# Compressed scores of an attention branch: keys held still on four column strips, scores turned back, and one low-weight subtraction moved behind two softmax steps

## The chip, the cores and the metric

The kernel runs on one core of one Trainium2 chip. TensorE multiplies matrices into PSUM, VectorE (DVE in the rows) and ScalarE (ACT) do elementwise work, GpSimd (POOL) some products, SyncE (SP) issues most transfers. The metric is the device time of one execution in microseconds. Before the change it is 2274.6 us, the median of three runs (2272.6 to 2280.66).

## The reference

Two transformer blocks over 256 tokens of width 1024. The first is a layer with three branches: a gated linear recurrence (A), a sparse attention (B), a gated linear attention (C). They are merged as

```
gates = sigmoid(merge_logit)                    # from h, one gate row per branch
merged = gates[0] * (y_a @ w_branch[0]) + gates[1] * (y_b @ w_branch[1]) + gates[2] * (y_c @ w_branch[2])
```

Branch B has 16 heads in 4 key groups, head width 64. For each head it sums three attentions: over the selected blocks, over the window, and over 15 compressed keys, which a small network makes from blocks of 32 tokens. The last one is what the change touches:

```
logit_c = einsum("bgrsd,bgcd->bgrsc", q, kc) + bias_c
p_c = softmax(where(valid_c, logit_c, NEG_INF)) * valid_c
o_cmp = einsum("bgrsc,bgcd->bgrsd", p_c, vc)
```

The second block (adaptive norms, two attention layers, gated feed-forward layers) is not touched.

## The kernel before

Each engine has one instruction stream, written out by hand, and the streams meet at semaphores. Weights are streamed into a ring in SBUF. A product of large weights is made in three passes of a one-pass type: ScalarE rounds a half chunk of 128x2048 weights to its high part (`w_hi`, L1656), VectorE subtracts to make the low part (`w_lo`, L2299), and TensorE multiplies high by high, high by low, low by high (`split_part`, L938 to L940). `rests_last` (L954, L955, L959) does the same 48 matmuls in another order: the 32 that need only the high weights come first, then a wait for the low weights, then the 16 with them.

Products in plain f32 (scores, turns, compressed network) leave two records each in the profile; a turn leaves one.

The stretch in question lies at 312 to 342 us. Branch C's last merge step, `mergeC3`, stands in the order after the start of branch B's attention (the postponed step): its half 0 is the gate logits (from h), its half 1 is y_c times w_branch. Around it:

- TensorE: small matmuls of the compressed network end (L1388 to L1410); `scores(0, 0)`, `scores(0, 1)` for unit 0 (L1281; a unit is a key group and a tile of 128 tokens); `compressed()` (L1423), 16 matmuls with the queries as the stationary 128x128 and only 14 or 30 key columns moving; `scores(1, 0)`, `scores(1, 1)`; `late_half(0, True)` by `split_part`; `late_half(1, False)` by `rests_last`; then the first turns and products of units 0 and 1 (L1326, L1352). `scores(1, 0)` may start when two of the four exponentials of unit 0 are through (`att_exp` at 2), `scores(1, 1)` at 4. The first product of L1352 waits until VectorE has emptied half 1 (`merged("C", 3)`).
- VectorE: `att_max(0)` (L2883, L2884), `w_lo` for half 0, `cmp_max(0)` and `cmp_max(1)` (L2914 to L2916: bias, maximum, subtraction), `att_max(1, (0,))` (L2877), `att_norm(0)` (L2936 to L2949), `w_lo` for half 1, `cmp_norm(0)` (L2923 to L2927), `att_max(1, (1,))`, `cmp_norm(1)`, `att_norm(1)`, `merged("C", 3)` (L2625, L2626), and then the next unit's `att_max`.
- ScalarE: exponentials of unit 0 (L2011), two `w_hi`, exponentials of the compressed scores (L2019), parts 0 and 1 of unit 1's exponentials, a table load and the sigmoid of the gate half (`late_gate`, L1853), a table load, parts 2 and 3 of unit 1's exponentials, which wait for `att_max(1, (1,))`.
- PSUM banks: raw scores of a unit 0 to 3, compressed scores 4, `late_half(0)` 5 and 6, `late_half(1)` 7 and 4.

Of the kernel before, what the change touches and what calls it, by code (L numbers as in the profile page):

```python
# [19 lines left out]
P = 128  # L20
D = 1024
KT = D // P
S = 256
# [10 lines left out]
CMP_N = S // 16 - 1  # L34
# [7 lines left out]
BANK = 512  # L42
# [275 lines left out]
def cmp_keys(t):  # L318

    return CMP_N if t else CMP_N // 2  # L320
# [17 lines left out]
def build(nc, d, out_x):  # L338
    f32 = mybir.dt.float32
    ACT = mybir.ActivationFunctionType  # L340
    ALU = mybir.AluOpType
    AX = mybir.AxisListType.X
    ctx = ExitStack()
    with ctx:
# [42 lines left out]
        def V(name, a=0, n=None):  # L387
            at, w = VOFF[name]
            return vec[:, at + a:at + (w if n is None else a + n)]
# [5 lines left out]
        def area(at, *shape):  # L395

            n = int(np.prod(shape))
            assert at + n <= ARENA, (at, shape)
            v = arena[:, at:at + n]
            if len(shape) == 2:  # L400
                return v.rearrange("p (a b) -> p a b", a=shape[0])
            if len(shape) == 3:
                return v.rearrange("p (a b c) -> p a b c", a=shape[0], b=shape[1])
            return v
# [8 lines left out]
        def cmp_scores(t):  # L413

            return psum[:, CMP_AT + cmp_col(t, 0):CMP_AT + cmp_col(t, 16)]

        def by_head(a):

            return a.rearrange("p (h c) -> p h c", h=16)
# [69 lines left out]
        def sig(name):  # L489
            if name not in sems:  # L490
                sems[name] = ctx.enter_context(nc.semaphore(name))
            return sems[name]
# [59 lines left out]
        B_pc = area(B_T_at + 4096, 16 * cmp_keys(0)), area(10916, 16 * cmp_keys(1))  # L552
        B_stat = [area(11156 + 16 * i, 16) for i in range(6)]
        B_hid = area(B_hid_at, 2, 2, 60)
        B_kd = V("wa2", 0, 8 * CMP_N).rearrange("p (g b c) -> p g b c", g=4, b=2)
        B_vc = area(10660, 4, HD)
        B_hT = rr[:, :].rearrange("p (i n) -> p i n", i=2)
        B_PT = area(16384, 3, BANK)
# [324 lines left out]
        def _(pe):  # L883
# [46 lines left out]
            def split_part(h, b, at, xh, xl, done, before=None, both=False, ks=None, between=None):  # L930

                wh, wl, nk = half_weights(h)
                ks = range(nk) if ks is None else ks
                for c, k in [(c, k) for k in ks for c in range(2)] if both else [(c, k) for c in range(2) for k in ks]:
                    if before is not None and c == 0:
                        before(k)
                    whc, wlc = wh[:, k, c * P:(c + 1) * P], wl[:, k, c * P:(c + 1) * P]
                    mm(b[c][:, at], whc, xh[:, k, at], start=(k == ks[0]), stop=False)  # L938
                    mm(b[c][:, at], whc, xl[:, k, at], start=False, stop=False)  # L939
                    last = mm(b[c][:, at], wlc, xh[:, k, at], start=False, stop=(k == ks[-1]))  # L940
                    if k == ks[-1] and done is not None:
                        last.then_inc(done, 1)
                    if k == ks[-1] and c == 0 and between is not None:
                        between()
# [320 lines left out]
            def scores(u, a):  # L1265
                kind, g, t = UNITS[u]

                def free(b):

                    if u > 0:  # L1270
                        pe.wait_ge(sig("att_exp"), 4 * (u - 1) + b + 1)

                if kind == "nsa":
                    nk = P * (t + 1)
                    free(1 + 2 * a)
                    for seg in range(2):
                        for r in (2 * a, 2 * a + 1):
                            half = slice(64 * (r % 2), 64 * (r % 2) + 64)
                            kk = (B_kk if g % 2 == r % 2 else B_ks)[half, 2 * seg + g // 2, 0:nk]
                            at = place(seg, r) * S  # L1280
                            last = mm(psum[:, at:at + nk], B_q[half, 2 * g + r // 2, t * P:(t + 1) * P], kk,  # L1281
                                      start=True, stop=True)
                else:
                    ev = kind == "ev"
                    k0 = S if t >= 2 else 0
                    for r in (2 * a, 2 * a + 1):
                        h = 4 * g + r
                        half = slice(64 * (r % 2), 64 * (r % 2) + 64)
                        free(r)
                        if ev:  # L1290
                            q = E_qk[half, h // 2, t * P:(t + 1) * P]
                            kk = (E_qk[half, 4, k0:TOK] if g == r % 2 else E_ks[half, k0:TOK])
                        else:
                            q = O_q[half, h // 2, t * P:(t + 1) * P]
                            kk = O_k[half, h // 2, 0:TOK]
                        last = mm(psum[:, r * BANK + k0:(r + 1) * BANK], q, kk, start=True, stop=True)  # L1296
                last.then_inc(sig("att_score"), 1)
# [117 lines left out]
                wait_evac(pe, TILE["cmp_kv"] + 1)  # L1415
                pe.wait_ge(sig("kswap_in"), 32)

            def compressed():
                for t in range(2):
                    sc = by_head(cmp_scores(t))  # L1420
                    for g in range(4):
                        for j in range(2):
                            last = mm(sc[:, 4 * g + j:4 * g + 4:2, :], B_q[:, 2 * g + j, t * P:(t + 1) * P],  # L1423
                                      B_kd[:, g, :, 0:cmp_keys(t)], start=True, stop=True)
                last.then_inc(sig("cmp_score"), 1)

            def late_half(half, both_parts):
                h = HALF_AT[f"mergeC3_{half}"]
                b = [late_tile(half, j) for j in range(2)]
                if both_parts:  # L1430
                    split_part(h, b, slice(0, S), h_hi, z_lo, filled)
                else:
                    pe.wait_ge(sig("cmp_exp"), 2)
                    rests_last(h, b, slice(0, S), C_yh, C_yl, filled)
# [1 line left out]
            nsa_ready()  # L1436
            scores(0, 0)
            scores(0, 1)
            compressed()
            scores(1, 0)  # L1440
            scores(1, 1)
            late_half(0, True)
            late_half(1, False)
# [831 lines left out]
        def _(dve):  # L2275
# [3 lines left out]
            def link(ins):  # L2279

                steps[0] += 1
                ins.then_inc(sig("dve_step"), 1)
                dve.wait_ge(sig("dve_step"), steps[0])
# [7 lines left out]
            def w_lo(h):  # L2291

                if h < lo_made[0] or h >= len(HALVES):
                    return
                assert h == lo_made[0]
                lo_made[0] += 1
                at = half_slot(h)
                dve.wait_ge(sig("w_hi"), h + 1)
                v.tensor_tensor(out=ring_r[:, at], in0=ring[:, at],  # L2299
                                in1=W_hi[h % NHI][:, 0:HALVES[h][2]].bitcast(f32), op=ALU.subtract)\  # L2300
                    .then_inc(sig("w_lo"), 1)
# [607 lines left out]
            def cmp_max(t):  # L2909
                n, nm = cmp_keys(t), B_stat[t]  # L2910
                sc = by_head(cmp_scores(t))
                bc = B_stage[:, :, 0:16 * (n - 1) + 1:16][:, :, ::-1]
                dve.wait_ge(sig("cmp_score"), 1)
                link(v.tensor_tensor(out=sc, in0=sc, in1=bc, op=ALU.add))  # L2914
                link(v.reduce_max(nm, sc, AX, negate=True))
                v.tensor_tensor(out=sc, in0=sc, in1=rep(nm, n), op=ALU.add).then_inc(sig("cmp_max"), 1)  # L2916

# [39 lines left out]
            def att_done(u, y):  # L2957
# [14 lines left out]

            link(v.memset(B_kd, 0.0))
            b = empty(TILE["cmp_kv"])
            v.tensor_copy(B_kd[0:64, :, 0, :], b[0:64, 0:60].rearrange("p (g c) -> p g c", g=4))
            v.tensor_copy(B_kd[64:128, :, 1, :], b[64:128, 0:60].rearrange("p (g c) -> p g c", g=4))\
                .then_inc(evac["V"], 1)
            b = empty(TILE["cmp_kv"] + 1)
            v.tensor_copy(B_vc[0:CMP_N, :, :], b[0:CMP_N, 0:256].rearrange("p (g d) -> p g d", g=4))\
                .then_inc(evac["V"], 1)  # L2980
            dve.wait_ge(sig("stage_in"), 16)
            att_max(0, (0, 1))
            w_lo(HALF_AT["mergeC3_0"])
            cmp_max(0)
            cmp_max(1)
            for u in range(0, NSA_U[1], 2):
                att_max(u + 1, (0,))
                att_norm(u, B_P, B_y)
                if u == 0:
                    w_lo(HALF_AT["mergeC3_1"])  # L2990
                    cmp_norm(0)
                att_max(u + 1, (1,))
                if u > 0:
                    att_done(u - 1, B_y)
                    if u + 2 < NSA_U[1]:
                        att_max(u + 2, (0,))
                    att_norm(u + 1, B_P, B_y)
                else:
                    cmp_norm(1)
                    att_norm(1, B_P, B_y)  # L3000
                    merged("C", 3, lambda j: late_tile(1, j))
                    att_max(2, (0,))
                    att_done(0, B_y)
                if u + 2 < NSA_U[1]:
                    att_max(u + 2, (1,))
                if u > 0:
                    att_done(u, B_y)
# [389 lines left out]
```

## Time and profile before

| | us |
|---|---|
| median of three runs | 2274.6 |
| the profiled execution | 2274.26 |
| its span, first to last instruction | 2272.5 |
| TensorE busy | 2240.5 (99%) |
| VectorE busy | 1456.9 (64%) |
| ScalarE busy | 929.2 (41%) |

The profile's busy time of TensorE runs to the modelled end of each matmul, so it says little on how full the array is; which engine sets the pace of a stretch is read from what each engine waits for there. The profile also lists the TensorE clock that was granted: 1.00 of full speed (2.4 GHz) in nearly the whole span, 0.50 (1.2 GHz) in one stretch, which is the one of this change.

### The profile page before, as it was taken

The numbers are of one execution on the slowest core, as the hardware profiler recorded it, in microseconds if no ns is written. First come the engines' busy times: TensorE is split into PE (matmuls) and PEld (weight loads), VectorE is DVE, ScalarE is ACT, GpSimd is POOL, SyncE is SP. The second block draws the span as 40 slices with busy tenths as digits, with TensorE's granted clock in tenths as the row PEclk, the third lists the DMA queues.
The fourth block names the chain that finished last, engine by engine and source line by source line (L and its number), as shares of the span: only waits on it lengthen the run. The fifth ranks groups of instructions, "written<-read, shape, count | busy, mean of one in ns | idle before, by whom it ended". The sixth has DMA issues, their size and how long they took to land.

```text
span 2272.5 us, 33457 instructions
## 1 busy us (share of the span) xinstructions
PE 2240.5 (99%) x14230; PEld 1958.4 (86%) x14230; DVE 1456.9 (64%) x1968; ACT 929.2 (41%) x1338; POOL 286.3 (13%) x254
## 2 busy tenths in 40 slices
PE   8999999999999999999999999999999999999999
PEld 8999986999998888888769888889888888978999
DVE  7674567788777767757858676326655332987554
ACT  7854447454552122234544212224322222556443
POOL 2020105121102010100110101000100101202111
PEclk9999999999999999999999999999999999999999
DMA  7553461756544545323213544223454321623553
GB/s 293 186 202 145 151 228 45 262 210 261 193 166 172 213 157 222 145 85 124 79 38 149 202 168 185 74 93 149 153 218 164 132 102 68 180 97 112 186 186 112
DMA packets 35728, 358.23 MB, mean 158 GB/s; under 512 B 4237, under 2 KB 6477, under 8 KB 9212
## 3 DMA queue, kind: packets, MB, share of 16 engines
q1 hardware_dynamic: 32124, 343.54, 40.3%
q0 software_dynamic: 3456, 12.56, 1.9%
q8 instruction: 112, 1.84, 0.3%
q14 instruction: 36, 0.29, 0.0%
HBM read 353.11 MB, written 1.13 MB: 156 GB/s over the span
## 4 chain that ended last, share of the span: by engine, by line
PE 91%; DVE 4%; ACT 3%; issue 1%; DMA 0%; POOLq 0%; ACTq 0%; DVEq 0%
PE psum L938 25%; PE psum L939 25%; PE psum L940 24%; PE psum L1031 2%; PE psum L1030 2%; PE psum L1029 2%; PE psum L959 1%; PE psum L954 1%; PE psum L955 1%; PE psum L1352 1%; PE psum L1326 1%; ACT arena_r L1656 1%; DVE ring_r L2299 1%; PE psum L1296 1%; PE psum L1281 1%
## 5 line engine op out<-in xcount | busy, mean ns | idle before, releaser
L938 PE MATMUL psum<-arena_r 128*128 128x256 f32 (+2 forms) x3032 | 1021.7, 337 | 4.5 <-DVE arena_r L2645 2.8
L940 PE MATMUL psum<-arena_r,ring_r 128*128 128x256 f32 (+2 forms) x3032 | 1015.5, 335 | 0.0
L1656 ACT ACTIVATE arena_r<-ring 128x2048 fp32r<-128x2048 f32 (+1 forms) x252 | 473.6, 1881 | 674.1 <-PE psum L940 619.9
L939 PE MATMUL psum<-zT_r,arena_r 128*128 128x256 f32 (+1 forms) x2240 | 741.3, 331 | 0.0
L2299 DVE TENSOR_TENSOR ring_r<-ring,arena_r 128x2048 fp32r<-128x2048 f32 (+1 forms) x251 | 569.0, 2269 | 187.7 <-ACT arena_r L1656 187.0
L938 PEld LDWEIGHTS psum<-arena_r 128*128 128x128 f32 x3032 | 570.6, 188 | 78.5 <-DVE ring_r L2299 4.1
L940 PEld LDWEIGHTS psum<-arena_r,ring_r 128*128 128x128 f32 x3032 | 573.0, 189 | 63.2
L939 PEld LDWEIGHTS psum<-zT_r,arena_r 128*128 128x128 f32 x2240 | 420.6, 188 | 41.8
L939 PE MATMUL psum<-arena_r 128*128 128x256 f32 (+2 forms) x1240 | 405.7, 327 | 0.0
L2455 DVE CUSTOM_DVE_ANT_0 psum<-arena,cb 128x1024 f32<-128x1024 f32 x256 | 315.7, 1293 | 0.0
L939 PEld LDWEIGHTS psum<-arena_r 128*128 128x128 f32 x1240 | 234.3, 189 | 22.2
L838 POOL TENSOR_TENSOR arena_r<-rt,arena_r 128x512 fp32r<-128x512 f32 (+1 forms) x55 | 81.7, 1486 | 990.6 <-ACT arena_r L1757 990.6
L2387 DVE SCALAR_TENSOR_TENSOR xT<-psum,gates_h,xT 128x256 f32<-128x256 f32 x168 | 75.4, 480 | 128.8 <-PE psum L940 128.0
L2521 DVE TENSOR_TENSOR rr<-psum,rr 128x512 f32<-128x512 f32 (+1 forms) x53 | 31.2, 590 | 175.4 <-PE psum L940 175.4
L2521 DVE TENSOR_TENSOR rt<-psum,rt 128x512 f32<-128x512 f32 (+1 forms) x53 | 31.3, 590 | 151.3 <-PE psum L940 149.5
L838 POOL TENSOR_TENSOR arena_r<-rr,arena_r 128x512 fp32r<-128x512 f32 (+1 forms) x55 | 78.7, 1432 | 343.6 <-ACT arena_r L1757 343.6
L938 PE MATMUL psum<-xT_r,arena_r 128*128 128x256 f32 x384 | 109.1, 284 | 0.7 <-DVE ring_r L2299 0.7
L940 PE MATMUL psum<-xT_r,ring_r 128*128 128x256 f32 x384 | 108.5, 283 | 0.0
L1031 PE MATMUL psum<-arena_r,zT_r 128*128 128x256 f32 x336 | 94.4, 281 | 0.0
L1029 PE MATMUL psum<-arena_r 128*128 128x256 f32 x308 | 87.8, 285 | 0.0
L1030 PE MATMUL psum<-ring_r,arena_r 128*128 128x256 f32 x308 | 86.3, 280 | 0.0
L1778 ACT ACTIVATE rt<-psum 128x512 f32<-128x512 f32 (+1 forms) x53 | 27.5, 519 | 139.0 <-PE psum L940 116.1
(386 smaller groups left out, 2470.7 us busy)
## 6 DMA issues: line engine op xcount, KB each, us to landing
ring<-in_wf SPq DMA_DIRECT2D x75, 2048.0 KB, 7.7
ring<-in_w SPq DMA_DIRECT2D x40, 2048.0 KB, 7.7
arena<-in_w SPq DMA_DIRECT2D x73, 1024.0 KB, 9.6
ring<-in_wf SPq DMA_DIRECT2D x10, 1536.0 KB, 6.4
ring<-in_w SPq DMA_DIRECT2D x6, 1024.0 KB, 8.7
arena<-strip_scratch POOLq DMA_DIRECT2D x1, 2048.0 KB, 10.4
arena<-rpb_scratch POOLq DMA_DIRECT2D x16, 128.0 KB, 10.7
xT<-in_x SPq DMA_DIRECT2D x1, 1024.0 KB, 7.1
```

The costliest lines, as they stand in the source:

```text
L838: pool.tensor_tensor(out=lo[:, i, :], in0=a, in1=hi[:, i, :].bitcast(f32), op=ALU.subtract)\
L938: mm(b[c][:, at], whc, xh[:, k, at], start=(k == ks[0]), stop=False)
L939: mm(b[c][:, at], whc, xl[:, k, at], start=False, stop=False)
L940: last = mm(b[c][:, at], wlc, xh[:, k, at], start=False, stop=(k == ks[-1]))
L1029: mm(b, xh[:, k, at], wh[:, k, :], start=(k == 0), stop=False)
L1030: mm(b, xh[:, k, at], wl[:, k, :], start=False, stop=False)
L1031: last = mm(b, xl[:, k, at], wh[:, k, :], start=False, stop=(k == nk - 1))
L1656: A(W_hi[h % NHI][:, 0:n], ring[:, half_slot(h)], ACT.Identity).then_inc(sig("w_hi"), 1)
L2299: v.tensor_tensor(out=ring_r[:, at], in0=ring[:, at], in1=W_hi[h % NHI][:, 0:HALVES[h][2]].bitcast(f32), op=ALU.subtract)\
L2387: return v.scalar_tensor_tensor(out=xT[:, k, at], in0=b[:, at], scalar=gate(k, s), in1=xT[:, k, at], op0=ALU.mult, op1=ALU.add)
L2455: v.tensor_tensor_reduce(out=psum[:, at:at + D], in0=src[:, b * D:(b + 1) * D], in1=cb[:, s * D:(s + 1) * D], scale=1.0, scalar=0.0, op0=A ...
L2521: v.tensor_tensor(out=a, in0=b[:, 0:nt], in1=a, op=ALU.mult).then_inc(evac["V"], 1)
```

## The change

Compressed scores. Instead of queries stationary and 14 or 30 key columns moving, each group's compressed keys become a stationary operand of 32 columns (two head parities by 16, the 16th key column zero), placed on column strip 32g of the array, and 256 tokens of queries move: 8 matmuls, into bank 7. The scores then lie keys by tokens. VectorE copies the bank to SBUF (`B_sc`, 128x512), TensorE turns it back in four 128x128 transposes into bank 7, and the addition of the bias reads from there, in two instructions for each token tile instead of one, and writes where the scores were before. In TensorE's order the turns come between `scores(1, 0)` and `scores(1, 1)`.

The postponed step. Half 0 uses `rests_last` instead of `split_part`, and VectorE makes its low weights after `cmp_max(0)`, `cmp_max(1)` and `att_max(1, (0,))` instead of before them.

```diff
-        B_kd = V("wa2", 0, 8 * CMP_N).rearrange("p (g b c) -> p g b c", g=4, b=2)
+        B_kd = V("wa2", 0, 8 * 16).rearrange("p (g b c) -> p g b c", g=4, b=2)
+        B_sc = area(24064, BANK)
+        cmp_flat = psum[:, 7 * BANK:8 * BANK]
...
-            def compressed():
+            def compressed_by_key():
+                for j in range(2):
+                    for g in range(4):
+                        last = mm(cmp_flat[32 * g:32 * g + 32, j * S:(j + 1) * S],
+                                  B_kd[:, g, :, :].rearrange("p b c -> p (b c)"), B_q[:, 2 * g + j, :],
+                                  start=True, stop=True, tile_position=(0, 32 * g))
+                last.then_inc(sig("cmp_by_key"), 1)
+
+            def compressed_turned():
+                pe.wait_ge(sig("cmp_copied"), 1)
                 for t in range(2):
-                    sc = by_head(cmp_scores(t))
-                    for g in range(4):
-                        for j in range(2):
-                            last = mm(sc[:, 4 * g + j:4 * g + 4:2, :], B_q[:, 2 * g + j, t * P:(t + 1) * P],
-                                      B_kd[:, g, :, 0:cmp_keys(t)], start=True, stop=True)
+                    for j in range(2):
+                        at = t * S + j * P
+                        last = nc.tensor.transpose(cmp_flat[:, at:at + P], B_sc[:, j * S + t * P:j * S + (t + 1) * P],
+                                                   C("ident"))
                 last.then_inc(sig("cmp_score"), 1)
...
-                    split_part(h, b, slice(0, S), h_hi, z_lo, filled)
+                    rests_last(h, b, slice(0, S), h_hi, z_lo, filled)
...
-            compressed()
+            compressed_by_key()
             scores(1, 0)
+            compressed_turned()
             scores(1, 1)
...
-                link(v.tensor_tensor(out=sc, in0=sc, in1=bc, op=ALU.add))
+                for j in range(2):
+                    at = t * S + j * P
+                    turned = cmp_flat[:, at:at + P].rearrange("p (h c) -> p h c", h=8)
+                    link(v.tensor_tensor(out=sc[:, j::2, :], in0=turned[:, :, 0:n], in1=bc[:, j::2, :], op=ALU.add))
...
             att_max(0, (0, 1))
-            w_lo(HALF_AT["mergeC3_0"])
+            dve.wait_ge(sig("cmp_by_key"), 1)
+            v.tensor_copy(B_sc, cmp_flat).then_inc(sig("cmp_copied"), 1)
             cmp_max(0)
             cmp_max(1)
             for u in range(0, NSA_U[1], 2):
                 att_max(u + 1, (0,))
+                if u == 0:
+                    w_lo(HALF_AT["mergeC3_0"])
                 att_norm(u, B_P, B_y)
```

## Rows read from the trace of the kernel before

**Rows 1.** The page, part 4: shares of the chain that ended last, by engine.
```profile
PE 91%; DVE 4%; ACT 3%; issue 1%; DMA 0%; POOLq 0%; ACTq 0%; DVEq 0%
```

**Rows 2.** Stretches: length; busy us of PE, PEld, DVE, ACT, POOL; granted clock; DMA.
```profile
312.60:316.30 3.70, 2.33 (x24) 1.82 (x24) 0.85 (x3) 2.19 (x5) 0.00 (x0) 1.00 0.96 319
...
317.40:320.00 2.60, 2.60 (x22) 2.59 (x20) 2.53 (x5) 2.59 (x9) 0.00 (x0) 0.83 1.00 429
320.00:322.85 2.85, 2.85 (x14) 2.80 (x14) 2.11 (x1) 2.85 (x11) 0.00 (x0) 0.50 1.00 425
...
326.28:328.00 1.72, 1.72 (x16) 1.72 (x15) 1.65 (x9) 1.11 (x5) 0.66 (x1) 1.00 0.02 5
```

**Rows 3.** Order of time, TensorE: start, us, line, operands, records, idle time before.
```profile
205.59 1.92 PE L1211 MATMUL psum<-arena 128*32 128x256 f32 x16
...
221.41 1.91 PE L1211 MATMUL psum<-arena 128*32 128x256 f32 x8
...
317.41 5.52 PE L1423 MATMUL psum<-vec,arena 128*128 128x14 f32 x32
322.86 3.49 PE L1281 MATMUL psum<-arena 64*128 64x256 f32 x16
...
326.29 0.39 PE L938 MATMUL psum<-xT_r,arena_r 128*128 128x256 f32 x1
...
337.73 0.60 PE L1326 MATMUL psum<-cst,arena 128*128 128x128 f32 x4
...
340.56 0.65 PE L1352 MATMUL psum<-arena 128*64 128x256 f32 x4 [0.57 <-DVE zT L2626]
...
343.54 1.14 PE L1281 MATMUL psum<-arena 64*128 64x256 f32 x8
344.61 0.66 PE L1326 MATMUL psum<-cst,arena 128*128 128x128 f32 x4
```

**Rows 4.** Order of time, VectorE, 319.8 to 340.1 us.
```profile
319.83 2.28 DVE L2299 TENSOR_TENSOR ring_r<-ring,arena_r 128x2048 fp32r<-128x2048 f32 x1
322.97 0.35 DVE L2914 TENSOR_TENSOR psum<-psum,arena 128x112 f32<-128x112 f32 x1 [0.86 <-PE psum L1423]
...
325.23 0.42 DVE L2877 CUSTOM_DVE_ANT_0 psum<-psum,arena 128x256 f32<-128x256 f32 x1
...
326.72 0.20 DVE L2936 RECIPROCAL small<-small 128x8 f32<-128x8 f32 x1
...
327.83 3.13 DVE L2299 TENSOR_TENSOR ring_r<-ring,arena_r 128x2048 fp32r<-128x2048 f32 x1
330.89 0.26 DVE L2923 TENSOR_REDUCE arena<-arena 128x16 f32<-128x112 f32 x1
...
333.66 0.14 DVE L2877 DVE_READ_ACCUMULATOR2_ANT small<- 128x1 f32 x1
333.66 0.40 DVE L2923 TENSOR_REDUCE arena<-arena 128x16 f32<-128x240 f32 x1
...
335.94 0.20 DVE L2936 RECIPROCAL small<-small 128x8 f32<-128x8 f32 x1 [0.50 <-ACT arena L2011]
...
340.09 0.42 DVE L2626 TENSOR_TENSOR zT<-zT,rt 128x256 f32<-128x256 f32 x1
```

**Rows 5.** Order of time, ScalarE: exponentials of units 0 and 1, a table load.
```profile
319.93 0.22 ACT L2011 ACTIVATION_READ_ACCUMULATOR arena<-psum,small 128x1 f32 x1
...
332.68 1.28 ACT L2011 ACT_TABLE_LOAD   x1
333.98 0.47 ACT L2011 ACTIVATE arena<-psum,small 128x256 f32<-128x256 f32 x1
```

**Rows 6.** Line 2914 alone: its two instructions, shortest, median, longest in ns.
```profile
L2914 DVE TENSOR_TENSOR psum<-psum,arena x2: 355/462/570, 323.0 to 323.9; 128x112 f32<-128x112 f32 x1, 128x240 f32<-128x240 f32 x1
```

**Rows 7.** Groups at 305 to 352 us: busy us, mean ns, idle before.
```profile
L2883 DVE TENSOR_TENSOR psum<-psum,arena 128x512 f32<-128x512 f32 x4 | 2.8, 693 | 0.9 <-PE psum L1281 0.9
L2967 DVE COPY arena<-psum 128x256 f32<-128x256 f32 x2 | 0.8, 425 | 2.4 <-PE psum L1352 2.4
```

More of the change, by code:

```diff
@@ L2974, in _ @@
             b = empty(TILE["cmp_kv"])
-            v.tensor_copy(B_kd[0:64, :, 0, :], b[0:64, 0:60].rearrange("p (g c) -> p g c", g=4))
-            v.tensor_copy(B_kd[64:128, :, 1, :], b[64:128, 0:60].rearrange("p (g c) -> p g c", g=4))\
+            v.tensor_copy(B_kd[0:64, :, 0, 0:CMP_N], b[0:64, 0:60].rearrange("p (g c) -> p g c", g=4))
+            v.tensor_copy(B_kd[64:128, :, 1, 0:CMP_N], b[64:128, 0:60].rearrange("p (g c) -> p g c", g=4))\
                 .then_inc(evac["V"], 1)
```

## The prediction

> **What bounds the kernel now.** First the page's chain: 91% of it is TensorE [rows 1], so over the span a microsecond off TensorE's path is a microsecond off the end. But the change lies in 20 us where the engines hand work to each other, so the stretch has to be read by itself. The table of stretches shows the granted clock there: at 312.6 to 316.3 us TensorE does little, at full clock; in the stretch from 317.4 the mean is 0.83, and from 320.0 on it is 0.50, the lower level of 1.2 GHz; at 326.28 it is 1.00 again [rows 2]. Before it fell the engine had stood nearly idle, then done unit 0's scores and half of the narrow matmuls of L1423.
>
> TensorE in order of time: L1423 from 317.41 to 322.86, 5.45 us; `scores(1, ...)` 3.4 us to 326.29, mostly at the lower clock; then 96 matmuls of the postponed step to 337.73, 0.119 us each; turns and scores; and at 340.56 the first product, for which TensorE waited on VectorE's L2626 [rows 3]. That wait ends the stretch: everything behind it on TensorE (`scores(2, 1)`), VectorE (`att_max(2)`) and ScalarE follows from it. So the question is what moves 340.51, the end of L2626 [rows 4].
>
> Back from there. L2626 ends 4.57 us after `att_norm(1)` begins at 335.94, and that began when ScalarE's exponentials of unit 1, begun at 333.98, were through: VectorE was idle 0.50 us before it [rows 4, 5]. Those exponentials wait for two things: the table load at 332.68, which ends at 333.96, and `att_max(1, (1,))`, which VectorE ended at 333.66 + 0.14 = 333.80 [rows 4, 5]. The first hangs on TensorE (the sigmoid needs the gate half, which ended near 332.0), and VectorE's line stood only 0.18 us behind it. Taking time from TensorE alone can gain next to nothing here; what adds over 0.18 us to VectorE's line is late at the end.
>
> **The change part by part.** (1) The compressed matmuls. 5.45 us of L1423 go. In their place are 8 f32 matmuls, 16 records, of 32 stationary columns and 256 moving. The nearest row is L1211, the same shape: 8 records on one strip take 1.91 us, 16 records on two strips 1.92 [rows 3], so two strips run beside each other. Bounds for 16 records over four strips: 3.8 us if all go in single file, 1.0 us if four go abreast; I take 1.0 to 1.9, so the end is at 318.4 to 319.3. Either way it is hidden, since `scores(1, 0)` cannot start until two exponentials of unit 0 are through, at 319.93 + 0.22 = 320.15 [rows 5], about 320.3 on TensorE. L1423 had covered that wait; now it lies open, and 5.45 us removed bring `scores(1, 0)` forward by 322.86 - 320.3 = 2.6 us.
>
> (2) The copy. VectorE is through with `att_max(0)` at 319.83, when its first subtraction began before [rows 4]. The copy of 128x512 out of PSUM has no row; a copy half as wide takes 0.43 us, an addition of the same width 0.69 [rows 7]. I take 0.69, as time follows width: done at 320.5. It could cost 0.43 at best. Queued behind it is `cmp_max`, which waits for the turns.
>
> (3) The turns. `scores(1, 0)` at full clock takes 344.61 - 343.54 = 1.07 us, four turns 0.66 [rows 3]: 320.3 + 1.07 + 0.66 = 322.0. VectorE begins `cmp_max` at 322.05 and not 322.97. It has stood idle for 1.5 us, where the subtraction of 2.28 us stood before.
>
> (4) `cmp_max` took 325.23 - 322.97 = 2.26 us [rows 4]. Each of its additions is now two. From 355 ns for 112 elements and 570 for 240 [rows 6] a line gives 1.68 ns an element and 167 ns fixed; one more fixed part and hand-over each time is 0.2 us, twice: 2.66 us, to 324.7. The bound below is nothing, if the fixed parts overlap.
>
> (5) `att_max(1, (0,))`, 326.72 - 325.23 = 1.49 us: to 326.2. Now the moved subtraction, 2.28 us as before, since no GpSimd work is beside it: to 328.5. (Beside GpSimd the other one takes 3.13 [rows 4], which is its bound above.) `att_norm(0)`, 1.11 us: 329.6. The second subtraction with GpSimd beside it, 3.06: 332.65. `cmp_norm(0)` and `att_max(1, (1,))`, 2.77 + 0.14: 335.55. So the exponentials begin at 335.6 and not 333.98, `att_norm(1)` at 335.6 + 1.96 = 337.6 and not 335.94, and L2626 ends at 342.1 and not 340.51: **+1.6 us**.
>
> The same in one line: copy 0.69, idle 1.53, second additions 0.4, less the idle 0.86 that is gone, less the slack 0.18, is +1.6.
>
> (6) TensorE meanwhile. The postponed step starts at about 323.1 and not 326.29, 3.2 us sooner. Its 32 high matmuls end at 323.1 + 3.8 = 326.9; then it waits until 328.5 for the low weights; the 16 last end at 330.4; half 1 (low weights there at 332.65) ends at 336.1, 1.6 us sooner than 337.73. `rests_last` delays the first of the gate's two tiles, but both sigmoids and the table load behind them still end near 332.6, ahead of 335.6. Then turns and scores until the third turn, which needs ScalarE's first copy, behind the exponentials, at 338.2; TensorE is out of work at 338.8 and stands until 342.1, 3.3 us against 0.57 before [rows 3]. All that TensorE saves is given back in this wait.
>
> (7) For nothing: B_kd's wider memset, the changed views of its copies, and the load that SyncE issues when half 1 ends, which comes sooner; no engine waits for these here.
>
> **The sum.** The profiled execution took 2274.26 us (span 2272.5), 0.3 below the median of 2274.6. With +1.6 it is 2275.9, on the median 2276.2. About 0.5%, 11 us, is what a measurement of this kernel can tell from no change: its three runs lie 8 us apart.
>
> **The rivals.** (A) The lower clock again falls on this stretch. For it: it did, and the idle time before 316.3 is untouched. Against: the narrow matmuls are gone. `scores(1, 0)` and the turns would take up to twice 1.73 us, so `cmp_max` begins 1.2 to 1.7 later: +2.8 to +3.3, 2277.7.
>
> (B) A second low stretch, slower. TensorE's new idle time of 3.3 us before 342.1 is nearly as long as that of 312.6 to 316.3, after which the clock fell. It decides if the clock falls before the dense work of unit 2. Price by the one such stretch: 16 records of scores took 3.4 us there against 2.1, so 1.3 us, and up to 3.4 if it lasts as long as before and all is TensorE's. On top of 1.6: 2277.5 to 2279.6. The Trainium skill, TensorE: Matmul & The Clock Gate, section "Why this matters for your kernels", warns that an idle gap between bursts of matmuls returns the clock to its lower level. By that rule (B), or (A), is what happens; the one fall in this trace agrees with it, since it follows the idle stretch, and the 0.57 us wait at 340.56 was followed by none.
>
> (C) The strips do not run beside each other, because four write one bank. Then 3.8 us, or about 5.9 if the clock falls midway: `cmp_max` begins 0.9 to 4.7 later than in (3), +2.5 to +6.3: up to 2280.9. Against: the two strips of L1211.
>
> (D) Faster: TensorE's line sets the end and not VectorE's. For it: the table load that bound ScalarE hung on TensorE, and a copy of 0.43, an addition split at no cost and a turn ready sooner each help. If all of VectorE's +1.6 were made up, the gain would be half 0's 1.6 us, at most the 3.2 by which the step starts sooner: 2271.4 to 2273.0. Against: 0.18 us of slack, and 1.5 us of idle VectorE in place of a hidden subtraction.
>
> **How the numbers follow.** Forecast (+1.6, full clock) 0.45; (A) 0.22; (B) 0.10; (C) 0.05; (D) 0.18. The range from 2271.3 to 2280.5 takes in (A), (B), nearly all of (C) and (D), and the scatter of a median of a few runs. None reaches 11 us either way, so within 0.5% has 0.95; faster 0.02 and slower 0.03 are for what no row shows.
>
> **What would show it.** Right: the eight matmuls end before 320; VectorE idle about 1.5 us ahead of L2914's successor; TensorE waiting once inside half 0 for the subtraction and about 3 us for L2626; the exponentials of unit 1's second half following `att_max` and no table load. Wrong: the first product of L1352 before 340.6, or a clock of 1.00 with `cmp_max` begun after 323. The prediction fails if VectorE's steps in (5) take other times than their rows, or if another part of the kernel, which the diff leaves alone, moves.

## The result

| | before | changed |
|---|---|---|
| median, us (22 runs each) | 2275.35 | 2279.12 |
| lowest to highest | 2272.22 to 2280.66 | 2276.25 to 2282.01 |
| span of the profiled execution | 2272.5 | 2276.0 |

The ratio is 1.0015, with a 95% interval of 1.0009 to 1.0021: by it the changed kernel is 3.4 us slower (2.0 to 4.8), which is within 0.5%; the medians lie 3.8 us apart. The forecast was 2276.2 (+1.6), its range 2271.3 to 2280.5. The median of the kernel before was 2275.35, 2276.39, 2276.86 and 2279.07 in the four sets of runs reported here, so versions are compared below by their ratio to the kernel before in the same set, and not by their medians.

VectorE in order of time in the changed kernel (start, us, line; in brackets the idle time before it and what ended it). These rows answer to [rows 4]:

```profile
319.42 0.68 DVE L2998 COPY arena<-psum 128x512 f32<-128x512 f32 x1
321.53 0.54 DVE L2928 TENSOR_TENSOR psum<-psum,arena 128x56 f32<-128x56 f32 x2 [1.43 <-PE psum L1433]
...
324.20 0.42 DVE L2888 CUSTOM_DVE_ANT_0 psum<-psum,arena 128x256 f32<-128x256 f32 x1
...
325.69 2.28 DVE L2310 TENSOR_TENSOR ring_r<-ring,arena_r 128x2048 fp32r<-128x2048 f32 x1
327.89 0.19 DVE L2950 RECIPROCAL small<-small 128x8 f32<-128x8 f32 x1
...
329.00 3.13 DVE L2310 TENSOR_TENSOR ring_r<-ring,arena_r 128x2048 fp32r<-128x2048 f32 x1
332.06 0.26 DVE L2937 TENSOR_REDUCE arena<-arena 128x16 f32<-128x112 f32 x1
...
336.97 0.20 DVE L2950 RECIPROCAL small<-small 128x8 f32<-128x8 f32 x1 [0.36 <-ACT arena L2022]
...
341.11 0.42 DVE L2637 TENSOR_TENSOR zT<-zT,rt 128x256 f32<-128x256 f32 x1
```

The subtraction that stood in the wait for the compressed scores (at 319.83 in [rows 4]) now stands at 325.69, and in its old place are a copy and 1.43 us of nothing. ScalarE, to be read against [rows 5]: its table is loaded at 330.65 and it then stands 3.07 us for `att_max`, where before the table was the later of the two.

```profile
330.65 1.28 ACT L2022 ACT_TABLE_LOAD   x1
335.00 0.47 ACT L2022 ACTIVATE arena<-psum,small 128x256 f32<-128x256 f32 x1 [3.07 <-DVE small L2888]
```

TensorE, to be read against [rows 3]:

```profile
317.01 1.07 PE L1423 MATMUL psum<-arena,vec 128*32 128x256 f32 x16
319.77 1.13 PE L1283 MATMUL psum<-arena 64*128 64x256 f32 x8 [1.69 <-ACT arena L2022]
320.83 0.66 PE L1433 MATMUL psum<-cst,arena 128*128 128x128 f32 x4
321.43 1.13 PE L1283 MATMUL psum<-arena 64*128 64x256 f32 x8
328.03 2.18 PE L961 MATMUL psum<-xT_r,ring_r 128*128 128x256 f32 x16 [1.47 <-DVE ring_r L2310]
...
336.87 1.30 PE L1328 MATMUL psum<-cst,arena 128*128 128x128 f32 x8
341.58 0.73 PE L1354 MATMUL psum<-arena 128*64 128x256 f32 x4 [3.42 <-DVE zT L2637]
...
343.40 2.17 PE L1354 MATMUL psum<-arena 128*64 128x256 f32 x8
...
346.54 2.08 PE L1283 MATMUL psum<-arena 64*128 64x256 f32 x8
```

The 32 narrow records of 5.52 us have become 16 of 1.07, and the engine has three new waits, the last of 3.42 us. Behind it the same instructions take nearly twice their time: 2.08 us for eight records of L1283, against 1.14 for L1281 in [rows 3], and 2.17 for eight of L1354, against 1.23 in the kernel before:

```profile
341.79 1.23 PE L1352 MATMUL psum<-arena 128*64 128x256 f32 x8
```

The table of stretches of the changed kernel says why (columns as in [rows 2]): the clock is 1.00 up to 342 and 0.57 on average from there to 350.

```profile
337.70:342.00 4.30, 0.88 (x8) 0.35 (x6) 4.23 (x6) 1.05 (x2) 2.76 (x1) 1.00 0.95 396
342.00:350.00 8.00, 8.00 (x41) 4.32 (x38) 3.88 (x12) 4.21 (x18) 0.00 (x0) 0.57 0.05 19
350.00:360.00 10.00, 9.66 (x79) 5.69 (x79) 6.84 (x22) 8.06 (x30) 3.27 (x2) 1.00 0.00 0
```

For all kernels below I cut the span at three events of TensorE: the first small turn of the compressed network (L1397 before, L1399 changed), the first product of unit 0 (L1352, L1354) and the first matmul of the merge of branch B (L938, L940). "Turn to product", for example, is the time from the first event to the second. The last column lists where the trace has the clock at 1.2 GHz, but for the last microseconds of the span.

| kernel | turn to product | product to merge B | merge B to the end | clock low, us |
|---|---|---|---|---|
| before | 27.50 | 45.96 | 1885.94 | 319.1 to 325.9 |
| changed | 28.92 | 48.74 | 1885.72 | 342.0 to 348.9 |

Of the changed kernel's 3.6 us more in its span, 1.42 lie before the first product and 2.78 behind it. The rest, -0.22 there and -0.40 ahead of the first turn, lies where the two kernels do the same.

### The profile page after: what moved, and what is told of

Same layout as the page of the kernel before. It is cut to its first block, busy times and chain, and to the rows that moved or that the text cites. A ratio compares the mean times of both kernels' runs of the same rounds, so it can differ in the third digit from the quotient of the medians.

```text
span 2276.0 us, 33436 instructions
## 1 busy us (share of the span) xinstructions
PE 2238.5 (98%) x14218; PEld 1954.0 (86%) x14218; DVE 1457.5 (64%) x1971; ACT 928.8 (41%) x1338; POOL 286.7 (13%) x254
## 4 chain that ended last, share of the span: by engine, by line
PE 91%; DVE 5%; ACT 3%; issue 1%; DMA 0%; POOLq 0%; ACTq 0%; DVEq 0%
PE psum L940 25%; PE psum L941 24%; PE psum L942 24%; PE psum L1033 2%; PE psum L1032 2%; PE psum L1031 2%; PE psum L961 1%; PE psum L956 1%; PE psum L957 1%; PE psum L1354 1%; DVE ring_r L2310 1%; PE psum L1328 1%; ACT arena_r L1667 1%; PE psum L1298 1%; PE psum L1283 1%
## 5 line engine op out<-in xcount | busy, mean ns | idle before, releaser
L940 PE MATMUL psum<-arena_r 128*128 128x256 f32 (+2 forms) x3032 | 1021.9, 337 | 4.5 <-DVE arena_r L2656 2.8
L940 PEld LDWEIGHTS psum<-arena_r 128*128 128x128 f32 x3032 | 570.5, 188 | 78.4 <-DVE ring_r L2310 4.1
L2466 DVE CUSTOM_DVE_ANT_0 psum<-arena,cb 128x1024 f32<-128x1024 f32 x256 | 315.6, 1291 | 0.5 <-DMA arena<-in_w 0.5
L940 PE MATMUL psum<-xT_r,arena_r 128*128 128x256 f32 x368 | 104.4, 284 | 0.7 <-DVE ring_r L2310 0.7
## 6 DMA issues: line engine op xcount, KB each, us to landing
arena<-strip_scratch POOLq DMA_DIRECT2D x1, 2048.0 KB, 10.2
```

What stands on the lines that cost most here:

```text
L2466: v.tensor_tensor_reduce(out=psum[:, at:at + D], in0=src[:, b * D:(b + 1) * D], in1=cb[:, s * D:(s + 1) * D], scale=1.0, scalar=0.0, op0=A ...
```

## The experiments

What stood against each other: the theory that VectorE's line sets the first product and the idle TensorE then loses its clock, and the theory that it is TensorE's own line (its waits inside the step, the work of unit 2).

**The gap filled.** In the changed kernel, ahead of the wait for the last merge:

```diff
                 if e == 0:
+                    pe.wait_ge(sig("att_exp"), 8)
+                    for i in range(24):
+                        mm(psum[:, 3 * BANK:3 * BANK + S], h_hi[:, i % KT, 0:P], h_hi[:, (i + 1) % KT, :],
+                           start=True, stop=True)
                     wait_evac(pe, TILE["mergeC3_1"] + 1)
```

> The changed kernel with 24 additional one-pass matmuls of 256 columns (about 0.12 us each, 2.8 us in all) into an unused PSUM bank, in the gap in which TensorE waits for VectorE's L2637 before the first product; their results are thrown away and the output is unchanged. Theory (idle stretch lowers the clock): the granted clock stays at 1.00 through 342 to 350 us, the end of L2637 stays where it is, and the kernel becomes 2 to 2.8 us faster than the changed one, about +1.4 us against the kernel before. Rival (the clock falls for the work of unit 2 itself, or the fall costs nothing because VectorE and ScalarE set the pace there): the fall stays, or the time stays within 0.5 us of the changed kernel.

Median 2277.94, ratio to before 1.0005 (0.9996 to 1.0013). TensorE in order of time, then the table of stretches:

```profile
339.48 3.12 PE L1477 MATMUL psum<-xT_r 128*128 128x256 f32 x24
343.14 0.65 PE L1354 MATMUL psum<-arena 128*64 128x256 f32 x4 [0.55 <-DVE zT L2641]
...
346.12 1.13 PE L1283 MATMUL psum<-arena 64*128 64x256 f32 x8
```

```profile
340.00:350.00 10.00, 8.98 (x70) 6.07 (x68) 8.54 (x22) 4.92 (x20) 2.48 (x2) 1.00 0.42 176
```

With only this filled, the clock stays up behind it and product to merge B takes 45.94 us, as in the kernel before (45.96). So the idle stretch, and not the work behind it, costs the 2.8 us. Turn to product was 29.44: in this execution the clock was low from 316.9 to 320.3, over unit 0's scores. That this earlier fall is what kept the later one away is ruled out by the step alone, below, which had both. By the ratios the kernel is 1.1 us slower than before (-0.9 to +3.0) where the changed one is 3.4 (2.0 to 4.8): about the 2 to 2.8 us between them that were expected, though the intervals overlap.

**The step alone.** The kernel before, with `rests_last` for half 0 and the late subtraction:

```diff
             att_max(0, (0, 1))
-            w_lo(HALF_AT["mergeC3_0"])
             cmp_max(0)
...
                 att_max(u + 1, (0,))
+                if u == 0:
+                    w_lo(HALF_AT["mergeC3_0"])
                 att_norm(u, B_P, B_y)
```

> The kernel before with the second part of the change alone (gate half by rests_last, its low weights behind att_max(1)). Theory (VectorE's line sets the end of the stretch): VectorE stands idle about 3.1 us before cmp_max instead of 0.86, and the end of the last merge comes 2.0 us later than in the kernel before (2.2 us of subtraction no longer hidden, less 0.18 of slack), 2 us on the whole kernel, about 4 if the clock falls as well. Rival (TensorE's line sets the end): no difference, since TensorE never waits for the low weights here.

Median 2279.22, ratio 1.0014 (1.0006 to 1.0023). VectorE and TensorE in order of time:

```profile
325.14 0.35 DVE L2914 TENSOR_TENSOR psum<-psum,arena 128x112 f32<-128x112 f32 x1 [4.98 <-PE psum L1423]
```

```profile
344.77 0.65 PE L1352 MATMUL psum<-arena 128*64 128x256 f32 x4 [2.00 <-DVE zT L2626]
```

VectorE is idle 4.98 us; more than 3.1 because the clock was low here from 315.7 to 329.4. A second profiled execution of the kernel before (below) had nearly the same low stretch, so the two can be compared. VectorE's wait there is 2.78 us, so 2.20 us of subtraction are laid open; turn to product is 31.96 against 30.54, +1.42. The other 0.8 us were hidden behind ScalarE's table load: VectorE stood 1.15 us for the exponentials ahead of `att_norm(1)` there, and 0.36 here. The rival expected no difference. Behind a wait of 2.00 us for L2626 the clock fell again, from 346.5 for 6.8 us, and product to merge B took 48.73, as in the changed kernel.

**The scores alone.** The changed kernel with `split_part` and the subtraction ahead of the copy:

```diff
             att_max(0, (0, 1))
+            w_lo(HALF_AT["mergeC3_0"])
             dve.wait_ge(sig("cmp_by_key"), 1)
             v.tensor_copy(B_sc, cmp_flat).then_inc(sig("cmp_copied"), 1)
...
-                if u == 0:
-                    w_lo(HALF_AT["mergeC3_0"])
```

> The kernel before with the first part of the change alone (compressed keys stationary on strips, scores turned back; the subtraction stays ahead of the copy, gate half by split_part). Theory (VectorE's line): the subtraction ends near 321.6, copy 0.7, turns 0.7, so cmp_max begins about 0.4 us later than before and its split additions add 0.35: +0.6 us for the end of the last merge, with 2 to 2.5 us of TensorE idle before the first product. Rival (TensorE's line): 1.5 to 3 us faster than before.

Median 2278.56, ratio 1.0009 (1.0000 to 1.0018): not faster, against the rival's 1.5 to 3 us. Turn to product is 29.17, +1.67 where I had +0.6, but the clock was low from 315.6 to 319.0 and again from 322.5 to 329.3, so this execution doesn't settle the size. TensorE's idle time before the product was 0.74 us and not 2 to 2.5, and product to merge B 45.94 with no fall.

**The subtraction behind the copy.** The changed kernel, one line moved:

```diff
             v.tensor_copy(B_sc, cmp_flat).then_inc(sig("cmp_copied"), 1)
+            w_lo(HALF_AT["mergeC3_0"])
...
-                if u == 0:
-                    w_lo(HALF_AT["mergeC3_0"])
```

> The changed kernel with the subtraction of the gate half directly behind the copy, so that it lies where VectorE waits for the turns. Theory (VectorE's line): the idle 1.4 us before cmp_max goes, TensorE does not wait inside half 0, and the last merge ends 1.4 us sooner than in the changed kernel, level with the kernel before; but TensorE is again idle for about 3 us before the first product, so the clock may fall again (+2). Rival (the wait of TensorE inside half 0, 1.5 us, is what costs): the same gain but no idle stretch at the product.

Median 2278.76, ratio 1.0010 (1.0001 to 1.0019). VectorE, then TensorE:

```profile
320.50 2.28 DVE L2310 TENSOR_TENSOR ring_r<-ring,arena_r 128x2048 fp32r<-128x2048 f32 x1
322.70 0.53 DVE L2928 TENSOR_TENSOR psum<-psum,arena 128x56 f32<-128x56 f32 x2
```

```profile
340.55 1.12 PE L1354 MATMUL psum<-arena 128*64 128x256 f32 x4 [3.42 <-DVE zT L2637]
```

VectorE has no idle time left before L2928, TensorE none inside half 0, and turn to product is 27.41: 1.5 us less than changed, as VectorE's line says. It is level with the 27.50 of the kernel before, but that execution had 6.8 us of low clock in this stretch and this one none. TensorE's wait before the product is 3.42 us all the same, the clock was low from 339.3 for 10.2 us, and product to merge B took 49.71. The saved time of TensorE only moves into this wait, and 1.0 of the 1.5 us was lost behind it by the longer low stretch; the unmoved kernel had one of 10.2 us as well in its second profile (49.63).

**The maxima of unit 1 ahead of cmp_norm(0).** On top of that:

```diff
-                    cmp_norm(0)
                 att_max(u + 1, (1,))
+                if u == 0:
+                    cmp_norm(0)
```

> The changed kernel with the subtraction behind the copy and att_max(1, (1,)) ahead of cmp_norm(0), but the last merge still behind att_norm(1). Theory (VectorE's line): the exponentials begin 1.3 us sooner, VectorE's idle 0.36 us before att_norm(1) goes, so the first product comes only 0.3 to 0.4 us sooner than with the subtraction behind the copy alone: most of the gain of the twice swapped kernel comes from the merge ahead of att_norm(1). Rival: the first product at about 337 already here.

Median 2277.39, ratio 0.9998 (0.9988 to 1.0008). Turn to product 26.96, 0.45 less; the wait is 3.44 us, the clock low for 10.2 us from 338.3, product to merge B 49.87.

**The last merge ahead of att_norm(1) as well.**

```diff
-                    att_norm(1, B_P, B_y)
                     merged("C", 3, lambda j: late_tile(1, j))
+                    att_norm(1, B_P, B_y)
```

> The changed kernel with the subtraction behind the copy and two further swaps on VectorE: att_max(1, (1,)) ahead of cmp_norm(0), and the last merge (merged C, 3) ahead of att_norm(1), so that it no longer stands behind the product that shares its path with GpSimd's. Theory (VectorE's line sets the end, and TensorE's saved time waits to be used): half 1 ends near 334.4, the merge runs 335.6 to 336.9, the first product starts near 337.1 instead of 340.5, 3.4 us sooner than with the subtraction behind the copy alone; TensorE is idle less than 1 us before it, so the clock does not fall there; 2 to 3.4 us faster than the kernel before. Rival (the order of att_norm(1) matters as much: the turns of unit 1 wait for it and the time comes back by unit 2): the first product comes sooner, but the stretch from it to the next merge grows by as much.

Median 2272.94 (2272.3 to 2274.17), ratio 0.9980 (0.9971 to 0.9989): by it 4.6 us faster than before (2.5 to 6.6), the first version that beats both kernels. VectorE, then TensorE:

```profile
335.45 0.43 DVE L2637 TENSOR_TENSOR zT<-zT,rt 128x256 f32<-128x256 f32 x1
...
336.24 0.42 DVE L2637 TENSOR_TENSOR zT<-zT,rt 128x256 f32<-128x256 f32 x1
```

```profile
336.72 0.65 PE L1354 MATMUL psum<-arena 128*64 128x256 f32 x4 [0.50 <-DVE zT L2637]
...
341.24 1.17 PE L1283 MATMUL psum<-arena 64*128 64x256 f32 x8 [1.47 <-ACT arena L2022]
```

L2637 takes 0.43 us where it took 1.67 beside a GpSimd product, and the first product comes 24.10 us after the first turn. Part of it comes back, as the rival said: product to merge B is 48.63, with a new wait of 1.47 us for unit 2's exponentials and 3.4 us at the low clock from 342.2.

**The same swap on the kernel before.** The last diff alone, on the kernel before.

> The kernel before with the last merge ahead of att_norm(1), nothing else. Half 1 ends at 337.7 here, so VectorE waits 2 us for it and merges by 339.1: first product 1.4 us sooner, but att_norm(1) 3.2 us later. Theory (TensorE's half 1 now sets it, which the change would bring forward): 0 to 1.4 us faster than before, clearly less than the same swap gives on the changed kernel. Rival (the swap does it all, the changed scores add nothing): as fast as the swapped changed kernel.

Median 2275.51, ratio 0.9991 (0.9981 to 1.0001), runs from 2270.52 to 2278.82. The profiled execution had the clock at full throughout the span: turn to product 23.59, product to merge B 46.71, span 2268.7. I had expected 337.7 for the end of half 1 by the row of before; at full clock it comes 3.7 us sooner. The granted clock is listed for every run. Where its mean is 1.000 this version took 2270.5 and 2270.7 us, the one with everything 2272.3 to 2272.9 (three runs): at equal clock the swap alone is not only as good, as the rival said, but 2 us better. What the version with everything has is a steadier clock: 0.998 to 1.000 over its 11 runs, which lie 1.9 us apart, against 0.996 to 1.000 here, 8.3 us apart. The two differ in the scores, in the step and in one more order on VectorE, so which of these steadies it isn't shown.

This profile shows one thing more. Up to the swap its program is the kernel before, so it has that kernel's line at full clock, VectorE and then ScalarE:

```profile
321.46 0.35 DVE L2914 TENSOR_TENSOR psum<-psum,arena 128x112 f32<-128x112 f32 x1
```

```profile
332.34 0.47 ACT L2011 ACTIVATE arena<-psum,small 128x256 f32<-128x256 f32 x1 [1.75 <-DVE small L2877]
```

The idle 0.86 us before L2914 and the wait for the table load that [rows 4] and [rows 5] have are both gone; they came with the low clock. Counted from the first turn, the exponentials of unit 1's second half begin at 19.84 us, against 20.92 in the profile of before and 22.34 in that of the changed kernel. In both of those the first product follows 6.58 us later, so the kernel before at full clock would have turn to product at 26.42: an estimate, 19.84 + 6.58. Against it the changed kernel's 28.92 is +2.5, and the 27.41 with the subtraction behind the copy is +1.0.

**Both kernels profiled again,** unchanged.

> The kernel before, unchanged, looked at once more. If the place at which the clock falls is bound to the program, its low stretch is again 319.1 to 325.9 us. If it is not (the changed kernel with and without filling fell at 342.0 and 316.9), it lies elsewhere or is longer, and the span changes with it by as much as the stretch is on TensorE's path: 0 to 4 us.

> The changed kernel, unchanged, looked at once more: the stretch up to the first product is again about 28.9 us if the clock is full in it; if the clock falls at unit 0's scores it is 29.4, as with the filled gap; the fall in the gap before the first product comes again (2.8 us more from the product to the next merge) if that gap is its cause.

The kernel before took 2279.13 us. TensorE:

```profile
316.96 2.08 PE L1281 MATMUL psum<-arena 64*128 64x128 f32 x16 [0.50 <-DVE arena L2979]
318.97 7.03 PE L1423 MATMUL psum<-vec,arena 128*128 128x14 f32 x32
```

Compare L1423's 5.52 us in [rows 3]: the clock was low from 316.8 for 13.7 us, and for 3.4 more at 463.6, outside this stretch. Turn to product was 30.54, merge B to the end 1887.12. The program is the same and the place of the fall is not. The changed kernel took 2279.92: turn to product 28.95 again, the wait before the product 3.42 us again, the clock low from 341.1 for 10.2 us, product to merge B 49.63.

**More waits filled.** Throw-away matmuls as in the first experiment. In the kernel before, 4, 3 and 4 in the three waits of the compressed network; in the twice swapped kernel those, 14 ahead of `scores(1, 0)` and 11 ahead of `scores(3, 0)`:

```diff
             compressed_by_key()
+            for f in range(14):
+                mm(psum[:, 6 * BANK + S:7 * BANK], h_hi[:, f % KT, 0:P], h_hi[:, (f + 1) % KT, :],
+                   start=True, stop=True)
             scores(1, 0)
```

> The kernel before with 4, 3 and 4 throw-away one-pass matmuls in the three waits of the compressed network (312.6 to 316.3 us), nothing else. Theory (the fall at unit 0's scores and at the narrow matmuls comes from the nearly idle stretch before them): the fall goes or comes later, runs gather at the fast end of the kernel before (2272), median 1 to 3 us faster. Rival (the narrow matmuls of L1423, 14 to 30 columns each, are what lowers it): the fall stays at about 319 and after, and the median and the scatter stay as they are.

> The twice swapped changed kernel with throw-away one-pass matmuls (36 in all, 0.12 us each, output unchanged) where TensorE waits: 4, 3 and 4 in the waits of the compressed network, 14 ahead of scores(1, 0), 11 ahead of the first scores of unit 3. Theory (idle TensorE lowers the clock, and the clock is the rest of the difference and of the scatter): no fall of the clock in 310 to 400 us, about 2 us faster than without them, near 2270.5, and runs that lie within 2 us of each other. Rival (these falls cost nothing, or the matmuls delay the real ones as much as they save): as fast as without them or slower.

The kernel before with its network filled: median 2274.93, ratio 0.9991 (0.9983 to 1.0000), 2272.2 to 2277.57. The fall is still there, later and shorter (3.4 us from 322.7), and turn to product 26.35. The listed clocks of the runs say more than this one profile: none of the 12 runs has a mean of 0.996, which 17 of the 29 runs of the kernel before in the same set have, all at 2278.6 us or more. So filling the nearly idle stretch took the longest falls away. The rival holds a part: with the stretch filled the clock still fell behind the narrow matmuls, though whether by them isn't shown, since the swap on the kernel before ran them at full clock with no fall. The swapped kernel filled: median 2272.69, ratio 0.9978 (0.9970 to 0.9987), 2271.89 to 2273.55. No fall in 310 to 400, product to merge B 47.22, 1.4 us less than unfilled; but the median hardly moved, and the profile shows a fall at 458.5 and 1887.38 us behind merge B. The 2 us that I expected did not come.

| kernel | turn to product | product to merge B | merge B to the end | clock low: from, for |
|---|---|---|---|---|
| before | 27.50 | 45.96 | 1885.94 | 319.1, 6.8 |
| before, again | 30.54 | 45.96 | 1887.12 | 316.8, 13.7; 463.6, 3.4 |
| changed | 28.92 | 48.74 | 1885.72 | 342.0, 6.8 |
| changed, again | 28.95 | 49.63 | 1885.95 | 341.1, 10.2 |
| gap filled | 29.44 | 45.94 | 1885.81 | 316.9, 3.4 |
| step alone | 31.96 | 48.73 | 1885.86 | 315.7, 13.7; 346.5, 6.8 |
| scores alone | 29.17 | 45.94 | 1887.43 | 315.6, 3.4; 322.5, 6.8; 462.4, 3.4 |
| subtraction behind copy | 27.41 | 49.71 | 1885.88 | 339.3, 10.2 |
| and maxima first | 26.96 | 49.87 | 1885.83 | 338.3, 10.2 |
| and merge first | 24.10 | 48.63 | 1885.87 | 342.2, 3.4 |
| merge first, on before | 23.59 | 46.71 | 1885.93 | none |
| twice swapped, filled | 24.02 | 47.22 | 1887.38 | 458.5, 3.4 |
| before, network filled | 26.35 | 45.94 | 1885.75 | 322.7, 3.4 |

## Why the prediction was right or wrong

**Right: VectorE's line, against the profile it was counted from.** The times are set against the first turn of the network, since the changed execution reached it 0.4 us sooner.
- (1) The 16 records took 1.07 us, four strips abreast, at the lower bound of 1.0 to 1.9; rival (C) is out. The wait for ScalarE lay open: `scores(1, 0)` stood 1.69 us for it.
- (2) The copy took 0.68 (0.69 taken). (3) VectorE stood 1.43 us (1.5).
- (4) `cmp_max` took 324.20 - 321.53 = 2.67 (2.66). (5) The subtraction took 2.28 (its successor starts after 2.20), `att_norm(0)` 1.11, the second subtraction 3.06 to its successor, all as their rows of before.
- The first product came 1.42 us later, where I had 1.6. The experiment that moves one line back gave 1.5 us back, and the step alone cost 1.42 at nearly equal low clock.
- (6) TensorE waited 1.47 us inside half 0 (1.6) and 3.42 before the product (3.3).

**Wrong: the clock left out of the sum.** The forecast of +1.6 was for a full clock, and (B), the second low stretch, had 0.10. The low stretch came in both profiles of the changed kernel, and with the 3.42 us wait also in the two versions that kept it; product to merge B was 2.8 to 3.9 us longer each time, and with the wait filled not at all. (B)'s price of 1.3 to 3.4 us on top was near it, its chance was far too low. It was to be seen in my own steps: I had found 3.3 us of idle TensorE and the row of one fall. My comparison with that row was loose: in the 3.70 us from 312.6 to 316.3 TensorE was busy for 2.33 [rows 2], so the new idle stretch was longer than any one wait there. The Trainium skill, TensorE: Matmul & The Clock Gate, section "Why this matters for your kernels", which I set beside it, was right that an idle gap between bursts of matmuls brings the clock down: the traces agree, with a fall behind the 3.42 us of idle TensorE in four profiles of four. They also have falls behind single waits of 2.00 us (the step alone) and 1.47 us (merge first), and none behind one of 0.97 us (the swap on the kernel before).

**Wrong: the time of before taken as one number.** I took the low stretch of [rows 2] as part of the kernel. It is part of an execution: the second profile had 13.7 us of it. Two terms of my sum, "less the idle 0.86 that is gone" and "less the slack 0.18", are effects of that low clock. At full clock the kernel before has neither, and the same sum gives 2.6 where the estimate above has +2.5. The agreement of 1.42 with 1.6 therefore holds for the two profiled executions and not for the two kernels at equal clock. (A), the same fall in the changed kernel, came in neither of its profiles, but did with the gap filled.

The measured 3.4 us can nearly be closed. Both first profiles have 6.8 us of low clock. In the kernel before it lies over the narrow matmuls and scores and costs 27.50 - 26.42 = 1.1 us, by the estimate; in the changed kernel it lies behind the first product and costs 2.8. That is 2.5 + 2.8 - 1.1 = 4.2 us for this pair, inside 2.0 to 4.8. What differs is VectorE's line and the place of the low stretch, not the amount of low clock: the mean listed clock is 0.9972 over the 85 runs of the kernel before beside the experiments and 0.9976 over the changed kernel's 22, and among runs listed at 0.998 the means are 2275.5 (29 runs) and 2278.7 us (13). Where the low stretches lie in the runs other than the profiled ones isn't shown.

That 2279.12 lies in the range is owed to its width, which was made for rivals, and not to the sum, which was 2.9 us short.

**Rival (D)** was wrong as it stood: TensorE's saved time never reached the end by itself. With VectorE merging first the kernel was 4.6 us faster than before, but the swap on the kernel before shows that the gain is the swap's and not that of the saved time: at equal clock it ends 2 us sooner without the changed scores. I had costed L2626's 1.67 us as fixed and had not asked why it takes four times the 0.42 of its twin at 340.09.

## What to carry to other kernels

Where engines hand work around, ask for each microsecond taken off one engine which wait it becomes; a subtraction that fills its own engine's wait is free there and costs its full time one step later. If a fall of the clock follows an idle stretch of TensorE in the trace at hand, give a new idle stretch of that kind the price of a fall, and take the clock out of both sides before subtracting one execution from the other: a wait in the profile of before may belong to its low clock and not to the kernel. Look for the instruction whose row is far longer than its twin's: its neighbour, not its own work, is what to move.

## What I had not expected of the hardware

- The same program has the clock low at different places and for different times: 6.8 us in one profile of the kernel before, 13.7 and 3.4 in the other. That goes with the 8 us between its fastest and slowest runs: those listed at a mean clock of 0.999 took 2272.8 us on average, those at 0.996 took 2279.6. The same 6.8 us cost 1.1 us (an estimate) in one place and 2.8 in another.
- Two elementwise operations of one shape on VectorE took 1.67 and 0.42 us. The long one started while GpSimd's 128x1024 product ran (336.50 to 339.44 in the profile of before); moved ahead of that product it took 0.43.
- Plain f32 matmuls on four column strips ran four abreast: 16 records of 256 columns in 1.07 us, where two strips took 1.92 and one strip as long for 8.
